# Per-block landing signals for x, and the last gate product taken ahead of the root, in a one-core decoder layer

## The chip, the cores and the metric

The kernel runs on one core of a Trainium2 chip. Its five engines are TensorE (PE, with its weight loads shown apart as PEld), VectorE (DVE), ScalarE (ACT), GpSimd (POOL) and SyncE (SP, which here only issues DMAs). The metric is the device time of one execution in microseconds; lower is better.

## The reference

One decoder layer on 512 tokens (four blocks of 128) of width 1024, in float32:

```
mod = silu(c) @ w_mod + b_mod            # six rows: shift, scale, gate for the mixer and for the FFN
h = rms_norm(x, pre_mix_gain) * (1 + scale_m) + shift_m
y = hybrid_mixer(h, ...)                 # differential attention beside a gated delta rule, one output projection
x = x + gate_m * rms_norm(y, post_mix_gain)
h = rms_norm(x, pre_ffn_gain) * (1 + scale_f) + shift_f
y = peer_ffn(h, ...)                     # 8 heads, product keys, top 16 of 16384 single-neuron experts
x = x + gate_f * rms_norm(y, post_ffn_gain)
```

Two places matter here. The first line with `rms_norm` needs the sum of squares of every row of x. The last line is, for each row, out = x1 + (y * gate) / sqrt(mean(y^2) + eps), where `gate` is gate_f times post_ffn_gain and x1 the x after the mixer.

## The kernel before

All buffers are placed by hand, every engine runs a program written out in order, and engines meet only at semaphores. The matrix products are float32 split in two parts (`hi`, `lo`), so each product is three matmuls.

**The start.** SP issues c (`c_row`), then the four blocks of x into `xn`, three small tables, and then weight tiles of 512 KB each in one stream: modulation tiles 0 to 3, input-projection tiles 0 and 1, modulation tiles 4 to 7, and so on. ACT takes silu(c), loads its table for the root, squares blocks 0 and 1 of x with the row sums kept (`ssq`); DVE squares blocks 2 and 3. All four x DMAs raise one semaphore, `s_x`, and both engines wait for its full count before the first square. ACT then takes the root of the means; DVE multiplies the first modulation tile (`mod_tile(0)`), inverts the roots, scales blocks 2 and 3, while ACT scales blocks 0 and 1. DVE goes on with modulation tiles 1 to 3 and from them makes the columns `acol`, `bcol` (`s_cols`). PE runs ten matmuls of the identity once block 0 is squared (`WARM`, waiting for `s_ssq`), then, when x is scaled, 32 transposes. ACT rounds the first weight tile (`hi(0)`, needs its DMA), copies two transposed column blocks out of PSUM (`x_copied(2)`, `x_copied(3)`) and makes h for the first two (`h_made`: a scale and a bias from `acol`, `bcol`, then a cast). DVE takes the remainders (`low`), and PE starts on the first natural tile of the input projection, 24 matmuls. Its end frees the weight slot for which ACT waits with `hi(2)`.

**The middle** is not touched: attention, delta rule, output projection, x1, retrieval beside the down projection of all 128 expert tiles, up projection of the same tiles for token blocks 0 to 2. Block 3 is done from 128 gathered rows per token on DVE (`ysp`).

**The end.** The blocks are finished in the order `FINISH` = (3, 0, 1, 2); block 3 lies in `ysp`, the other three in two PSUM banks each. PE ends with the last two expert tiles, one bank after the other, and signals each bank with `s_yb`. ACT squares the two halves of a block with row sums (`out_square`) and takes the root when DVE has the mean. DVE does, for each block in `finish(n)`, the following; the two halves are 512 columns each:

```
tt(rstd, ssq2 half 0, ssq2 half 1, add); drain; ts(rstd, 1/D, EPS) -> s_ym     # the mean of squares
wait s_yr; reciprocal(rstd); drain                                             # ACT's root between
for half in range(2):
    stt(yo = y * rstd * gate_f); drain; tt(yo = yo + x1) -> s_yo
```

SP stores blocks 3, 0 and 1 with one DMA of 512 KB each, and block 2 with one of 256 KB for each half.

Of the kernel before, what the change touches and what calls it, by code (L numbers as in the profile page):

```python
# [26 lines left out]
F32 = mybir.dt.float32  # L27
# [4 lines left out]
ALU = mybir.AluOpType  # L32
# [3 lines left out]
P = 128  # L36
D = 1024
SEQ = 512
KD = D // P
NB = SEQ // P  # L40
# [29 lines left out]
NG = NB - 1  # L70
# [24 lines left out]
def build(nc, x, c, mod_tiles, mod_bias_col, gain_cols, in_tiles,  # L95
# [6 lines left out]
    with ExitStack() as ctx:  # L102
        def sem(name):
            return ctx.enter_context(nc.semaphore(name))
# [4 lines left out]
        def at(name, shape, dt, offset=None):  # L109
            size = 2 if dt == BF16 else 4  # L110
            for n in shape[1:]:
                size *= n
            offset = cursor[0] if offset is None else offset
            cursor[0] = offset + (size + 31) // 32 * 32
            assert cursor[0] <= 229344, (name, cursor[0])
            return nc.alloc_sbuf_tensor_at(name, shape, dt, offset=offset)
# [11 lines left out]
        gate_f = at("gate_f", [P, D], F32)  # L128
# [6 lines left out]
        phase = cursor[0]  # L135


        xn = at("xn", [P, NB, D], F32)
# [83 lines left out]
        rstd = small[:, 8:12]  # L222
# [26 lines left out]
        bank = [ctx.enter_context(nc.psum_tensor(f"bank{i}", [P, 512], F32)) for i in range(8)]  # L249
# [43 lines left out]
        asp = at("asp", [P, P], F32)  # L293
        assert cursor[0] <= phase + 32 * 1024
        rows = at("rows", [P, ROWS, D], F32, phase + 32 * 1024)
        x1 = at("x1", [P, NB, D], F32, late)
        yo = at("yo", [P, NB, D], F32)
        ysp = at("ysp", [P, D], F32)
# [5 lines left out]
        s_hi = sem("split_hi_ready")  # L304
        s_lo = sem("split_lo_ready")
        s_used = sem("split_used")
        s_x = sem("x_landed")
        s_crow = sem("c_landed")
        s_c = sem("consts_landed")
        s_hc = sem("head_consts_landed")  # L310
# [120 lines left out]
        s_yq = sem("y_squares")  # L431
        s_yqa = sem("y_first_half_squares")
        s_ym = sem("y_mean_square")
        s_yr = sem("y_root")
        s_yo = [sem(f"out_ready{b}") for b in range(NB)]
        s_out = sem("out_stored")
# [18 lines left out]
        def _(sp):  # L455
            dq = sp.dma_start
            dq(c_row[:], c.partition_broadcast(P)).then_inc(s_crow, 16)
            for b in range(NB):
                dq(xn[:, b, :], x[b]).then_inc(s_x, 16)
            for dst, src in [(gaincol[:], gain_cols), (modbcol[:], mod_bias_col), (baw[:], ba_w)]:  # L460
                dq(dst, src).then_inc(s_c, 16)

# [229 lines left out]
        def _(act):  # L692
# [12 lines left out]
            sc.activation(gate_f[:], c_row[:], ACT.Silu).then_inc(s_cc, 1)  # L705
            act.wait_ge(s_pool, 1)
            sc.activation(rx[:, 0:1], eps_t, ACT.Sqrt)
            act.wait_ge(s_x, 16 * NB)
            for b in range(2):
                sc.activation(qkvT[:, 0:2, :], xn[:, b, :].rearrange("p (a n) -> p a n", a=2),  # L710
                              ACT.Square, accum_out=ssq[:, b:b + 1]).then_inc(s_ssq, 1)
                act.wait_ge(s_ssq, b + 1)
# [347 lines left out]

            def out_square(b, half):
                w = slice(half * 512, (half + 1) * 512)
                return sc.activation(yo[:, b, w], ysp[:, w] if b == NG else bank[2 * b + half][:],
                                     ACT.Square, accum_out=ssq2[:, 2 * b + half:2 * b + half + 1])

            for n, b in enumerate(FINISH):
                for half in range(2):
                    if b < NG:
                        act.wait_ge(s_yb, NB - 1 + 2 * b + half + 1)
                    elif half == 0:  # L1070
                        act.wait_ge(s_axpy, PICKS)
                    last = out_square(b, half)
                last.then_inc(s_yq, 1)
                act.wait_ge(s_ym, NB + n + 1)
                sc.activation(rstd[:, b:b + 1], rstd[:, b:b + 1], ACT.Sqrt).then_inc(s_yr, 1)
# [468 lines left out]
        def _(dve):  # L1544
# [65 lines left out]
                tt(wlo[:, n % SPLIT, :], raw[:, n % RAW, :], whi[:, n % SPLIT, :].bitcast(F32),  # L1610
                   ALU.subtract).then_inc(s_lo, 1)

            dve.wait_ge(s_x, 16 * NB)
            for b in range(2, NB):
                v.tensor_tensor_reduce(out=qkvT[:, 2 * b:2 * b + 2, :].rearrange("p a n -> p (a n)"),
                                       in0=xn[:, b, :], in1=xn[:, b, :], scale=1.0, scalar=0.0, op0=ALU.mult,
                                       op1=ALU.add, accum_out=ssq[:, b:b + 1]).then_inc(s_xsd, 1)
# [540 lines left out]

            def finish(n):
                b = FINISH[n]  # L2160
                dve.wait_ge(s_yq, NB + n + 1)
                tt(rstd[:, b:b + 1], ssq2[:, 2 * b:2 * b + 1], ssq2[:, 2 * b + 1:2 * b + 2], ALU.add)
                v.drain()
                ts(rstd[:, b:b + 1], rstd[:, b:b + 1], 1.0 / D, EPS, ALU.mult, ALU.add).then_inc(s_ym, 1)
                dve.wait_ge(s_yr, NB + n + 1)
                v.reciprocal(rstd[:, b:b + 1], rstd[:, b:b + 1])
                v.drain()
                for half in range(2):
                    w = slice(half * 512, (half + 1) * 512)
                    stt(out=yo[:, b, w], in0=ysp[:, w] if b == NG else bank[2 * b + half][:],  # L2170
                        scalar=rstd[:, b:b + 1], in1=gate_f[:, w], op0=ALU.mult, op1=ALU.mult)
                    v.drain()
                    last = tt(yo[:, b, w], yo[:, b, w], x1[:, b, w], ALU.add)
                    if half == 1 or n == NB - 1:
                        last.then_inc(s_yo[b], 1)

# [64 lines left out]
```

## Time and profile before

| | |
|---|---|
| time, median of 3 runs | 2153.97 us (2153.74 to 2157.31) |
| the profiled execution: own time | 2165.47 us |
| the profiled execution: span from first to last instruction | 2163.4 us |
| busy: PE, PEld, DVE, ACT, POOL | 82%, 66%, 58%, 33%, 40% |
| mean granted TensorE clock | 0.882 of full speed |
| moved by DMA | 376.21 MB, mean 174 GB/s |

The span is 2.1 us shorter than the execution's own time, and that execution was 11.5 us longer than the median. In a row of a timeline the columns are: start and duration in us, engine, line of the kernel, operation, output and inputs with their shapes, how many instructions are merged, and in brackets how long the engine had been idle and what ended that.

### The profile page before, as it was taken

The page shows a single profiled execution, that of the slowest core. Times are in us where ns is not written, and L with a number is a line of the kernel's source. Part 1 is how long each engine was busy: PE and PEld are TensorE (multiplying, and loading weights), DVE is VectorE, ACT ScalarE, POOL GpSimd, SP SyncE. Part 2 cuts the span into 40 slices and gives each one's busy share as a digit, 9 for nine tenths or more (in the row PEclk, how much of TensorE's full clock was granted, in tenths as well). Part 3 has the DMA queues.
Part 4 walks back from the last instruction along what each step waited for, and adds up shares of the span by engine and source line. Part 5 has one row for each costly group of instructions (what it writes and reads, how often), then busy time and mean ns, then how long its engine had stood idle before and what let it go on. Part 6 is the DMA issues. An engine that isn't in the chain of part 4 may idle for free.

```text
span 2163.4 us, 25624 instructions
## 1 busy us (share of the span) xinstructions
PE 1772.3 (82%) x7938; PEld 1419.9 (66%) x7938; DVE 1254.9 (58%) x3054; ACT 704.1 (33%) x1048; POOL 855.5 (40%) x708
## 2 busy tenths in 40 slices
PE   7999899899962279622797227999999999999998
PEld 5776698788841168411585115888888888888886
DVE  7788764316952068610676205722226888888886
ACT  4435654423410034100341002444323333333333
POOL 0332023231077700777007771010005767677750
PEclk9999899999975589755797557999999999999999
DMA  8722913223610034100342003464458999999994
GB/s 344 272 69 95 418 42 108 107 78 127 222 60 15 1 117 146 61 13 15 102 149 69 15 15 102 146 222 142 136 174 286 351 371 360 374 344 372 377 377 160
DMA packets 149363, 376.21 MB, mean 174 GB/s; under 512 B 32048, under 2 KB 64944, under 8 KB 146096
## 3 DMA queue, kind: packets, MB, share of 16 engines
q1 hardware_dynamic: 114480, 308.04, 39.9%
q0 software_dynamic: 34816, 67.41, 8.7%
q8 instruction: 25, 0.41, 0.1%
q14 instruction: 42, 0.34, 0.1%
HBM read 312.25 MB, written 63.11 MB: 174 GB/s over the span
## 4 chain that ended last, share of the span: by engine, by line
PE 76%; issue 17%; DVE 5%; ACT 2%; DMA 1%; DVEq 1%; SPq 0%; ACTq 0%
PE bank L1091 14%; PE bank L1093 14%; PE bank L1092 14%; PE bank L1511 8%; PE bank L1509 8%; PE bank L1513 8%; PE bank L1286 1%; PE bank L1301 1%; DVE modr L1583 1%; PE bank L1469 1%; DVE small L1710 0%; PE bank L1311 0%; DMA xn<-in_x 0%; PE bank L1424 0%; PE bank L1422 0%
## 5 line engine op out<-in xcount | busy, mean ns | idle before, releaser
L1092 PE MATMUL bank<-act_lo,whi 128*128 128x512 f32 x1312 | 530.6, 404 | 115.9 <-issue 115.2
L1093 PE MATMUL bank<-act_hi,wlo 128*128 128x512 f32 x1312 | 529.8, 404 | 115.2 <-issue 114.6
L1091 PE MATMUL bank<-act_hi,whi 128*128 128x512 f32 x1312 | 533.4, 407 | 110.3 <-issue 107.6
L658 POOL DMA_INDIRECT gate_scratch<-merged,idx_cell x384 | 388.3, 1011 | 415.0 <-DVE cand L2039 294.6
L1974 DVE TENSOR_TENSOR wlo<-raw,whi 128x1024 fp32r<-128x1024 f32 x254 | 310.3, 1222 | 411.1 <-ACT whi L1005 365.1
L1093 PEld LDWEIGHTS bank<-act_hi,wlo 128*128 128x128 f32 x1312 | 255.8, 195 | 190.8 <-issue 141.5
L1092 PEld LDWEIGHTS bank<-act_lo,whi 128*128 128x128 f32 x1312 | 256.2, 195 | 185.2 <-issue 137.2
L1091 PEld LDWEIGHTS bank<-act_hi,whi 128*128 128x128 f32 x1312 | 255.8, 195 | 183.6 <-issue 133.6
L1509 PE MATMUL bank<-whi,chi 128*128 128x512 f32 x768 | 298.8, 389 | 0.0
L1511 PE MATMUL bank<-wlo,chi 128*128 128x512 f32 x768 | 298.8, 389 | 0.0
L1513 PE MATMUL bank<-whi,clo 128*128 128x512 f32 x768 | 298.8, 389 | 0.0
L1011 ACT ACTIVATE aout<-bank 128x512 f32<-128x512 f32 x128 | 76.6, 599 | 602.0 <-PE bank L1093 290.9
L667 POOL DMA_INDIRECT asp<-act_scratch,idx_act x128 | 163.1, 1274 | 255.3 <-DMA act_scratch<-aout 216.5
L676 POOL DMA_INDIRECT rows<-in_expert_tiles,idx_row x128 | 176.1, 1376 | 197.8 <-DVE gsp L2017 99.9
L602 POOL TENSOR_TENSOR wlo<-raw,whi 128x1024 fp32r<-128x1024 f32 x38 | 95.8, 2524 | 240.3 <-ACT whi L702 240.3
L1040 ACT CAST chi<-coef 128x384 fp32r<-128x384 f32 x128 | 65.6, 513 | 322.9 <-PE bank L1513 163.2
L2135 DVE SCALAR_TENSOR_TENSOR ysp<-rows,csp,ysp 128x1024 f32<-128x1024 f32 x127 | 163.3, 1286 | 12.1 <-issue 0.4
L1509 PEld LDWEIGHTS bank<-whi,chi 128*128 128x128 f32 x768 | 144.1, 188 | 30.0
L1513 PEld LDWEIGHTS bank<-whi,clo 128*128 128x128 f32 x768 | 144.1, 188 | 29.9
L1511 PEld LDWEIGHTS bank<-wlo,chi 128*128 128x128 f32 x768 | 144.1, 188 | 29.9
L2039 DVE SCALAR_TENSOR_TENSOR cand<-esp,pick 128x128 f32<-128x128 f32 x384 | 113.0, 350 | 79.0 <-issue 77.2
L1005 ACT CAST whi<-raw 128x1024 fp32r<-128x1024 f32 x128 | 133.5, 1043 | 1.0 <-DMA raw<-in_expert_tiles 0.7
(357 smaller groups left out, 1868.9 us busy)
## 6 DMA issues: line engine op xcount, KB each, us to landing
raw<-in_expert_tiles SPq DMA_DIRECT2D x256, 512.0 KB
act_scratch<-aout SPq DMA_DIRECT2D x128, 256.0 KB
gate_scratch<-zeros SPq DMA_DIRECT2D x24, 1024.0 KB, 22.0
a_in<-act_scratch SPq DMA_DIRECT2D x128, 192.0 KB
g_in<-gate_scratch SPq DMA_DIRECT2D x128, 192.0 KB
modr<-in_mod_tiles SPq DMA_DIRECT2D x28, 512.0 KB
raw<-in_in_tiles SPq DMA_DIRECT2D x28, 512.0 KB
raw<-in_query_tiles SPq DMA_DIRECT2D x16, 512.0 KB
```

What stands on the lines that cost most here:

```text
L658: g.indirect_dma_start(out=gate_cells, out_offset=bass.IndirectOffsetOnAxis(ap=idx_cell[:, b, k:k + 1], axis=0), in_=merged[:, b, k:k + 1] ...
L667: g.indirect_dma_start(out=asp[:, k:k + 1], out_offset=None, in_=act_cells, in_offset=bass.IndirectOffsetOnAxis(ap=idx_act[:, k:k + 1], ax ...
L676: g.indirect_dma_start(out=rows[:, k % ROWS, :], out_offset=None, in_=expert_rows, in_offset=bass.IndirectOffsetOnAxis(ap=idx_row[:, k:k + ...
L1005: sc.copy(whi4[:, n % WSLOT, :], raw[:, n % RAW, :]).then_inc(s_hi, 1)
L1091: mm(out_bank[:], whi[:, slot, w], act_hi[:, k, :], start=(k == 0), stop=False)
L1092: mm(out_bank[:], whi[:, slot, w], act_lo[:, k, :], start=False, stop=False)
L1093: last = mm(out_bank[:], wlo[:, slot, w], act_hi[:, k, :], start=False, stop=(k == KD - 1))
L1509: mm(o, chi[:, j % WSLOT, a], whi4[:, j % WSLOT, w], start=start, stop=False, skip_group_check=True)
L1511: mm(o, chi[:, j % WSLOT, a], wlo4[:, j % WSLOT, w], start=False, stop=False, skip_group_check=True)
L1513: return mm(o, clo[:, j % WSLOT, a], whi4[:, j % WSLOT, w], start=False, stop=stop, skip_group_check=True)
L1974: tt(wlo4[:, n % WSLOT, :], raw[:, n % RAW, :], whi4[:, n % WSLOT, :].bitcast(F32), ALU.subtract).then_inc(s_lo, 1)
L2135: stt(out=ysp[:], in0=rows[:, k % ROWS, :], scalar=c, in1=ysp[:], op0=ALU.mult, op1=ALU.add).then_inc(s_axpy, 1)
```

## The change

Two parts. At the start, `s_x` becomes four semaphores, one for each block of x, and each square waits for its own block alone. At the end, DVE first multiplies y by the gate (`by_gate`), the first half as soon as ACT has squared that half (new semaphore `s_ysq`), the second half between handing over the mean and waiting for the root; then one operation for each half multiplies by the inverse root and adds x1. ACT's squares, whose elements nobody reads, go to `ysq`, which lies over the gathered rows, and no longer to `yo`.

```diff
+        ysq = at("ysq", [P, NB, D], F32, phase + 32 * 1024)
...
-                dq(xn[:, b, :], x[b]).then_inc(s_x, 16)
+                dq(xn[:, b, :], x[b]).then_inc(s_x[b], 16)
...
-            act.wait_ge(s_x, 16 * NB)
             for b in range(2):
+                act.wait_ge(s_x[b], 16)
                 sc.activation(qkvT[:, 0:2, :], xn[:, b, :].rearrange("p (a n) -> p a n", a=2),
...
                     last = out_square(b, half)
+                    if half == 0:
+                        last.then_inc(s_ysq, 1)
...
-            dve.wait_ge(s_x, 16 * NB)
             for b in range(2, NB):
+                dve.wait_ge(s_x[b], 16)
                 v.tensor_tensor_reduce(out=qkvT[:, 2 * b:2 * b + 2, :].rearrange("p a n -> p (a n)"),
...
                 b = FINISH[n]
+
+                def by_gate(half):
+                    w = slice(half * 512, (half + 1) * 512)
+                    tt(yo[:, b, w], ysp[:, w] if b == NG else bank[2 * b + half][:], gate_f[:, w], ALU.mult)
+
+                dve.wait_ge(s_ysq, n + 1)
+                by_gate(0)
                 dve.wait_ge(s_yq, NB + n + 1)
                 tt(rstd[:, b:b + 1], ssq2[:, 2 * b:2 * b + 1], ssq2[:, 2 * b + 1:2 * b + 2], ALU.add)
                 v.drain()
                 ts(rstd[:, b:b + 1], rstd[:, b:b + 1], 1.0 / D, EPS, ALU.mult, ALU.add).then_inc(s_ym, 1)
+                by_gate(1)
                 dve.wait_ge(s_yr, NB + n + 1)
                 v.reciprocal(rstd[:, b:b + 1], rstd[:, b:b + 1])
                 v.drain()
                 for half in range(2):
                     w = slice(half * 512, (half + 1) * 512)
-                    stt(out=yo[:, b, w], in0=ysp[:, w] if b == NG else bank[2 * b + half][:],
-                        scalar=rstd[:, b:b + 1], in1=gate_f[:, w], op0=ALU.mult, op1=ALU.mult)
-                    v.drain()
-                    last = tt(yo[:, b, w], yo[:, b, w], x1[:, b, w], ALU.add)
+                    last = stt(out=yo[:, b, w], in0=yo[:, b, w], scalar=rstd[:, b:b + 1], in1=x1[:, b, w],
+                               op0=ALU.mult, op1=ALU.add)
```

DVE's instructions for block 2, the last to be finished, before; `small` holds the sums, means and roots, and what stands in brackets is the semaphore waited for:

```order
L2162 TENSOR_TENSOR small<-small 128x1 [waits y_squares]
L2164 TENSOR_SCALAR small<-small 128x1
L2166 RECIPROCAL small<-small 128x1 [waits y_root]
L2170 SCALAR_TENSOR_TENSOR yo<-bank,small,gate_f 128x512
L2173 TENSOR_TENSOR yo<-yo,x_150 128x512
L2170 SCALAR_TENSOR_TENSOR yo<-bank,small,gate_f 128x512
L2173 TENSOR_TENSOR yo<-yo,x_150 128x512
```

The same place after the change (lines are four to nine further on; a drain is no row):

```order
L2168 TENSOR_TENSOR yo<-bank,gate_f 128x512 [waits y_half_squared]
L2173 TENSOR_TENSOR small<-small 128x1 [waits y_squares]
L2175 TENSOR_SCALAR small<-small 128x1
L2168 TENSOR_TENSOR yo<-bank,gate_f 128x512
L2178 RECIPROCAL small<-small 128x1 [waits y_root]
L2182 SCALAR_TENSOR_TENSOR yo<-yo,small,x_151 128x512 x2
```

There are four wide instructions as before. Two of them now stand ahead of the reciprocal, one ahead of the sum, and the last two follow each other with no drain between.

ACT's first rows after the change, at the start of the program, where only the waits of the two squares (`qkvT,small<-xn`) are new:

```order
L709 ACT_TABLE_LOAD
L709 ACTIVATE small<-small 128x1 [waits pool_consts]
L712 ACTIVATE qkvT,small<-xn 128x1024 [waits x_landed0]
L712 ACTIVATE qkvT,small<-xn 128x1024 [waits x_landed1,sum_of_squares]
L716 ACTIVATE small<-small 128x4 [waits x_squared_then_scaled_by_vector,sum_of_squares]
L719 ACTIVATE xn<-xn,small 128x1024 [waits inverse_root]
```

No instruction moved there; the first square waits for block 0 of x, the second for block 1, where both had waited for all four.

## Rows read from the trace of the kernel before

**Rows 1.** The page's chain of work that ended last, shares of the span.

```profile
PE 76%; issue 17%; DVE 5%; ACT 2%; DMA 1%; DVEq 1%; SPq 0%; ACTq 0%
```

**Rows 2.** That chain in order of time: start us, us, what.

```profile
2.61 7.97 DMA xn<-in_x
...
30.77 0.04 ACT whi L702
```

**Rows 3.** The four DMAs of x (line L459), from issue to landing.

```profile
DMA to landing us min/median/max: 5.3/6.6/8.0
```

**Rows 4.** Timeline, the first 24 us.

```profile
10.60 1.06 ACT L710 ACTIVATE qkvT<-xn 128x1024 f32<-128x1024 f32 x1 [3.02 <-DMA xn<-in_x]
...
11.75 1.22 DVE L1615 CUSTOM_DVE_ANT_0 qkvT<-xn 128x1024 f32<-128x1024 f32 x1
...
11.89 4.59 PE L1113 MATMUL bank<-ident 128*128 128x128 f32 x20 [11.89 <-ACT qkvT L710]
...
12.90 1.22 DVE L1583 CUSTOM_DVE_ANT_0 modr<-modr,gate_f 128x1024 f32<-128x1024 f32 x1
...
16.49 3.48 PEld L1118 LDWEIGHTS bank<-ident,xn 128*128 128x128 f32 x32 [0.29 <-ACT xn L717]
...
17.19 1.05 ACT L702 CAST whi<-raw 128x1024 fp32r<-128x1024 f32 x1 [0.75 <-DMA raw<-in_in_tiles]
...
18.14 1.07 ACT L722 COPY qkvT<-bank 128x512 f32<-128x512 f32 x2
...
19.57 0.16 DVE L1593 SCALAR_TENSOR_TENSOR acol<-acol,gaincol 128x2 f32<-128x2 f32 x1
...
19.90 0.78 ACT L732 ACTIVATE wk<-bank,bcol,acol 128x512 f32<-128x512 f32 x1 [0.69 <-PE bank L1118]
...
23.48 0.76 PE L1104 MATMUL bank<-whi,act_hi 128*128 128x512 f32 x1 [3.27 <-issue]
```

**Rows 5.** Windows: from:to, length, busy us of PE, PEld, DVE, ACT, POOL, clock, DMA share, GB/s.

```profile
20.30:23.40 3.10, 0.00 (x0) 0.00 (x0) 1.97 (x4) 3.04 (x5) 0.00 (x0) 0.96 1.02 408
23.40:27.00 3.60, 3.52 (x9) 2.83 (x10) 3.60 (x6) 2.29 (x6) 0.00 (x0) 0.56 1.03 411
```

**Rows 6.** Timeline of PE behind an idle stretch later on.

```profile
393.12 5.93 PE L1459 MATMUL bank<-ident,xs 128*128 128x128 f32 x28 [6.03 <-DVE xs L1951]
```

**Rows 7.** Timeline of DVE at the end, first of block 0, then of block 2.

```profile
2149.62 0.16 DVE L2162 TENSOR_TENSOR small<-small 128x1 f32<-128x1 f32 x1 [4.16 <-ACT yo L1063]
...
2157.14 0.15 DVE L2162 TENSOR_TENSOR small<-small 128x1 f32<-128x1 f32 x1
...
2157.80 0.16 DVE L2166 RECIPROCAL small<-small 128x1 f32<-128x1 f32 x1 [0.27 <-ACT small L1075]
2158.03 0.75 DVE L2170 SCALAR_TENSOR_TENSOR yo<-bank,small,gate_f 128x512 f32<-128x512 f32 x1
2158.86 0.69 DVE L2173 TENSOR_TENSOR yo<-yo,x 128x512 f32<-128x512 f32 x1
2159.47 0.75 DVE L2170 SCALAR_TENSOR_TENSOR yo<-bank,small,gate_f 128x512 f32<-128x512 f32 x1
2160.29 0.69 DVE L2173 TENSOR_TENSOR yo<-yo,x 128x512 f32<-128x512 f32 x1
```

**Rows 8.** Timeline of ACT at the end, the squares of block 1 and 2, second halves.

```profile
2151.62 0.60 ACT L1063 ACTIVATE yo<-bank 128x512 f32<-128x512 f32 x1 [0.67 <-PE bank L1513]
...
2154.49 0.59 ACT L1063 ACTIVATE yo<-bank 128x512 f32<-128x512 f32 x1
```

**Rows 9.** Timeline of DVE in the mixer's own norm, where x1 is made.

```profile
371.59 0.16 DVE L1912 TENSOR_TENSOR small<-small 128x1 f32<-128x1 f32 x1 [2.02 <-ACT osq L957]
371.83 0.15 DVE L1914 TENSOR_SCALAR small<-small 128x1 f32<-128x1 f32 x1
371.90 0.68 DVE L1924 TENSOR_TENSOR xs<-bank,gate_m 128x512 f32<-128x512 f32 x1
372.49 0.15 DVE L1918 RECIPROCAL small<-small 128x1 f32<-128x1 f32 x1
```

More of the change, by code:

```diff
@@ L306, in build @@
         s_used = sem("split_used")
-        s_x = sem("x_landed")
+        s_x = [sem(f"x_landed{b}") for b in range(NB)]
         s_crow = sem("c_landed")
@@ L433, in build @@
         s_ym = sem("y_mean_square")
+        s_ysq = sem("y_half_squared")
         s_yr = sem("y_root")
@@ L1062, in out_square @@
                 w = slice(half * 512, (half + 1) * 512)
-                return sc.activation(yo[:, b, w], ysp[:, w] if b == NG else bank[2 * b + half][:],
+                return sc.activation(ysq[:, b, w], ysp[:, w] if b == NG else bank[2 * b + half][:],
                                      ACT.Square, accum_out=ssq2[:, 2 * b + half:2 * b + half + 1])
```

## The prediction

> **What bounds the kernel now.** I read the page's chain first. PE carries three quarters of it and DVE a twentieth [rows 1], so for most of the run a faster DVE is worth nothing. The change touches only the first and last dozen microseconds, so those two ends are read on their own.
>
> At the start the chain in order of time begins with the landing of x, from 2.61 to 10.58 us [rows 2]. ACT had been idle for 3.02 us when it began its first square at 10.60 [rows 4]. From there the chain runs through DVE (squares, modulation tiles, columns), ACT's h, DVE's remainder, and PE's first tile of the input projection at 23.48 [rows 4], and it comes back to ACT's rounding of weight tile 2 at 30.77, which waits for the end of that tile [rows 2]. Behind it engines wait for engines, and I found no wait for a stream of tiles that keeps its own time up to the attention stage; a shift of this start should therefore reach the end of the run.
>
> At the end PE is done at about 2154.3, when ACT takes the last square [rows 8], but DVE works on until 2160.98 [rows 7], and the last store can only be issued then. DVE waits 4.16 us for the squares of block 0 and is then busy without a gap but 0.27 us for each root [rows 7]. The end is DVE's.
>
> **The start, part by part.** The four x DMAs take 5.3 to 8.0 us to land [rows 3]; they were issued one after the other, the first at about 1.2 and the last at 2.6. The first thus lands at 6.5 and the last at 10.6, and as they share one stream I put the other two at even steps between, 7.9 and 9.2 (an estimate). Nothing about the DMAs changes. ACT is free at 7.58 (10.60 - 3.02) [rows 4], squares block 0 at 7.6 and block 1 at 8.8. DVE can square block 2 at 9.2 and block 3 from 10.6 to 11.8; before, that second square began at 11.75 [rows 4]. So DVE's chain is 1.15 us earlier: its first modulation tile would start at 11.75 where it was 12.90 [rows 4]. That tile may land a little later than that. Five tiles, the last of them the projection tile for which ACT waits at 17.19 [rows 4], land between 10.6 and 17.1, some 1.3 us each, which puts the first at 11.9. So I take 1.0 us for DVE's lead; bounds 0.5 (a tile that lands late) and 1.15.
>
> Not all of it comes through. The columns are finished at 19.73 (19.57 + 0.16), and ACT begins h at 19.90, after 0.69 us idle [rows 4]. The row puts this down to PE's transposes, but the bank that it needs was done long before; it is the columns. With these at 18.7, ACT is the late one: its rounding at 17.19 waits for its DMA [rows 4], which does not move, and the two copies behind it end at 19.21 [rows 4]. So h starts at 19.2, and the gain is that 0.69 us, with 0.3 us of DVE's lead left over. PE's first tile starts at 22.8. Bounds of this term: 0 (something that I take for hidden is not) and 0.7.
>
> **TensorE's clock at the start.** PE's ten identity matmuls (20 passes) take 4.59 us, 0.23 each, and the 32 transposes behind them 3.48, 0.11 each [rows 4]: PE was at 1.2 GHz, and at 2.4 GHz once the transposes began. Then it was idle 3.27 us [rows 4]; the granted clock reads 0.96 in that stretch and 0.56 in the next [rows 5], which is 1.2 GHz for about 3.3 us. A projection matmul then starts every 0.43 us and later every 0.23; seven or eight of them cost 1.5 us. The change moves the warm-up and not in step with the rest. It waits for block 0's square, now done at 8.7 and not at 11.8, so it runs from 8.8 to 13.4; the transposes, which wait for the scaling, only come 1.0 us earlier, at 15.5. A hole of 2.1 us opens in work that had been without one, and the idle stretch ahead of the first tile grows from 3.27 to about 3.6 us. I take it that neither changes a level: the hole is shorter than the stretch that did, and the first tile runs at 1.2 GHz as before. Term 0; bounds minus 1.5 (a first tile at 2.4 GHz) and plus 3.3 (all its 24 matmuls at 1.2 GHz: 24 x 0.20 = 4.8, less the 1.5 that it loses already).
>
> The Trainium skill, TensorE: Matmul & The Clock Gate, in the part on the HAM clock gate, says that the slow level is the default, that activity releases it and idling brings it back. The granted clock of the idle stretch agrees. By that rule a warm-up that is cut off from its work is partly wasted, and this speaks against the early signal; the second rival below prices it from rows.
>
> **The end, part by part.** Before, a block takes DVE from sum to sum 3.76 us: sum to reciprocal 0.66 with the wait for the root, 0.23 to the first product, 0.83 (drained) to the sum with x1, 0.61 to the second product, 0.82, 0.61 [rows 7]. After, the steps are priced by the mixer's norm, which already has this pattern: sum to mean 0.24, mean to gate product 0.07, product out of PSUM to reciprocal 0.59, with the root already there [rows 9]; reciprocal to the next wide one 0.23 [rows 7]. The two combined operations are not in the trace with a wide one behind them and no drain. They are of the kind of 0.75 us [rows 7], and the undrained one of 0.69 is followed after 0.61 [rows 7], so I take 0.75 - 0.08 = 0.67. With the first gate product at 0.60, a block takes 0.60 + 0.24 + 0.07 + 0.59 + 0.23 + 0.67 + 0.67 = 3.07 us. Is another engine late then? The sum of block 0 waits for ACT's square as before, at 2149.62, and its first gate product fits under ACT's second square. Blocks 0, 1 and 2 end at 2149.62 + 2.47 + 3.07 + 3.07 + 0.08 = 2158.3. ACT's square of block 1's second half ends at 2152.3 and is wanted at 2152.7; that of block 2 ends at about 2155.1 and is wanted at 2155.8 [rows 8]. So DVE stays the bound, 2.7 us earlier than 2160.98. Behind it come the same two stores of 256 KB; they are now issued 0.7 us apart, where it was 1.4, and may queue for 0.1 us. Bounds for the end: 1.9 (the first rival) and 2.8. Block 3 is finished under PE's last matmuls and costs nothing.
>
> **Sum.** 0.7 at the start and 2.7 at the end are 3.4 us: the profiled execution would have a span of 2160.0 and an own time of 2162.1. That execution was 11.5 us over the median, but the two ends are priced by durations that do not hang on it, so I take the 3.4 off the median: 2153.97 - 3.4 = 2150.6 us, or 0.16%. Less than 0.2% (4.3 us) is about what a measurement of this kernel can't tell from no change.
>
> **Rivals.** First, the drain is not what costs. The Trainium skill, VectorE: DVE Perf Modes, Rules for kernel authors, says that an operation waits for the pipe behind the one before it whatever one writes, and that only their number counts; the number of wide ones is unchanged here. The rows speak against it, 0.82 with a drain and 0.61 without [rows 7], though for two kinds of operation. As a mechanism: the combined operations keep 0.82. A block then takes 3.37 us and not 3.07, the end gives 1.9, and the time is 2151.4. Chance 0.08.
>
> Second, the hole costs the clock and gives it back: the transposes run at 1.2 GHz. A transposition pass at that level took 5.93 / 28 = 0.21 us [rows 6]. The four groups that ACT needs then end at 15.5 + 16 x 0.21 = 18.9, the copy behind them at 19.6, and the start gives 0.3. But the transposes end at 21.5 or later, PE is idle under 2 us, and the first tile runs at 2.4 GHz: 1.5 more. Sum 0.3 + 1.5 + 2.7 = 4.5, time 2149.5. Chance 0.25. Close to it, with 0.08: the transposes stay fast and the clock doesn't fall before the first tile, 4.9, 2149.1.
>
> Third, the start gives nothing, since a tile or the ACT queue is later than I read: only the end's 2.7, time 2151.3. Chance 0.12.
>
> Fourth, on the other side: the hole keeps PE at 1.2 GHz through the transposes and the whole first tile. Then the start gives 0.3 and costs 3.3, the end gives 2.7, and the time is 2154.3; if the low level lasts into the second tile, each matmul there adds 0.2, and 20 of them make it slower by over 0.2%. It decides as soon as the low level outlasts the first tile. Against it: 7 us of unbroken transposing raised or held the clock here. Chance 0.05.
>
> **How the numbers follow.** The forecast has 0.42, the rest is above. Faster by over 0.2% needs 4.3 us: most of the second rival and its neighbour, and what a scatter of a microsecond or more (the three runs differ by 3.6) adds to the forecast: 0.32. Slower: half of the fourth rival and a slow draw, 0.05. The rest, 0.63, is within 0.2%. The range takes in 2149.1 and 2154.3, with that scatter on the lower side: 2146.8 to 2154.4.
>
> **What would show it.** Right: ACT's first square at about 7.6 and the PE warm-up at 8.8; h at 19.2 and the first projection matmul at 22.8; at the end, gate products under the squares, no idle time before the reciprocals, 3.1 us from sum to sum, 8.7 us from block 0's sum to the last element where it was 11.36. Wrong: transposes at 0.21 a pass, a first tile at another level than before, a 0.8 step between the combined operations, or a middle between 31 and 2147 us whose length has changed by more than a microsecond: then clock or queues elsewhere, not this change's terms, decide the measured difference.

## The result, and the profile after

| | before | after |
|---|---|---|
| median of 12 runs each | 2154.83 us (2144.95 to 2163.83) | 2151.6 us (2114.15 to 2158.68) |
| the profiled execution: own time | 2165.47 us | 2150.9 us |
| its span | 2163.4 us | 2149.1 us |
| mean granted TensorE clock | 0.882 | 0.887 |

The ratio after to before is 0.9864, with a 95% interval of 0.9824 to 0.9903: faster by 1.0 to 1.8%. The medians of all twelve runs differ by 3.2 us, which is 0.15% and close to the 3.4 us forecast. The ratio and the medians don't agree because the ratio counts only three of the changed kernel's twelve runs (2114.15, 2127.27 and 2135.65), the others lying more than 1.5% above the fastest. The mean of these three lies 27 us below that of the other nine, and the first question is whether that has anything to do with the change.

The start is seen in the timeline of the changed kernel's first 24 us (start, duration, engine, line, operation, idle time before), the counterpart of [rows 4].

```profile
7.76 1.04 ACT L712 ACTIVATE qkvT<-xn 128x1024 f32<-128x1024 f32 x1
...
9.04 4.60 PE L1117 MATMUL bank<-ident 128*128 128x128 f32 x20 [9.04 <-ACT qkvT L712]
...
10.59 1.23 DVE L1619 CUSTOM_DVE_ANT_0 qkvT<-xn 128x1024 f32<-128x1024 f32 x1
...
12.23 1.23 DVE L1587 CUSTOM_DVE_ANT_0 modr<-modr,gate_f 128x1024 f32<-128x1024 f32 x1 [0.41 <-DMA modr<-in_mod_tiles]
...
15.83 3.71 PE L1122 MATMUL bank<-ident,xn 128*128 128x128 f32 x32 [2.19 <-ACT xn L719]
...
18.16 1.06 ACT L724 COPY qkvT<-bank 128x512 f32<-128x512 f32 x2
...
18.90 0.16 DVE L1597 SCALAR_TENSOR_TENSOR acol<-acol,gaincol 128x2 f32<-128x2 f32 x1
...
19.24 0.78 ACT L734 ACTIVATE wk<-bank,bcol,acol 128x512 f32<-128x512 f32 x1
...
22.82 0.47 PE L1108 MATMUL bank<-whi,act_hi 128*128 128x512 f32 x1 [3.28 <-issue]
```

The squares start with their own blocks. The first modulation tile comes 0.67 us earlier than before, not 1.0, for DVE now waits 0.41 us for its DMA. The columns are done at 19.06 and ACT's copies at 19.22, so h starts at 19.24 and the first projection matmul at 22.82, 0.66 us earlier than before. PE has the forecast hole of 2.19 us behind its warm-up. Its transposes take 3.71 us, and took as long before: the 3.48 us of [rows 4] are those of the weight loads (PEld, 3.48 us in both traces), and PE's own row in the kernel before is this one.

```profile
16.50 3.71 PE L1118 MATMUL bank<-ident,xn 128*128 128x128 f32 x32
```

The end is seen in DVE's timeline of the changed kernel, of block 0, the sum of block 1, and block 2, the counterpart of [rows 7].

```profile
2137.99 0.16 DVE L2173 TENSOR_TENSOR small<-small 128x1 f32<-128x1 f32 x1 [0.67 <-ACT ysq L1065]
2138.23 0.15 DVE L2175 TENSOR_SCALAR small<-small 128x1 f32<-128x1 f32 x1
2138.30 0.68 DVE L2168 TENSOR_TENSOR yo<-bank,gate_f 128x512 f32<-128x512 f32 x1
2138.90 0.15 DVE L2178 RECIPROCAL small<-small 128x1 f32<-128x1 f32 x1
2139.13 1.42 DVE L2182 SCALAR_TENSOR_TENSOR yo<-yo,small,x 128x512 f32<-128x512 f32 x2
...
2141.06 0.15 DVE L2173 TENSOR_TENSOR small<-small 128x1 f32<-128x1 f32 x1
...
2144.12 0.15 DVE L2173 TENSOR_TENSOR small<-small 128x1 f32<-128x1 f32 x1
...
2145.02 0.15 DVE L2178 RECIPROCAL small<-small 128x1 f32<-128x1 f32 x1
2145.25 1.41 DVE L2182 SCALAR_TENSOR_TENSOR yo<-yo,small,x 128x512 f32<-128x512 f32 x2
```

From sum to sum it is 3.07 and 3.06 us, no reciprocal waits for its root, and from block 0's sum to the last element it is 8.67 us (2145.25 + 1.41 - 2137.99) where it was 11.36. This is the forecast to a hundredth or two.

The middle did not repeat. I cut each trace at PE's matmuls number 3000 (about 604 us in), 4400 and the last, by their starts in the timeline:

| us | start to 3000 | 3000 to 4400 | 4400 to the last | last to the end |
|---|---|---|---|---|
| before | 606.2 | 747.8 | 799.9 | 9.5 |
| after | 603.7 | 738.6 | 799.9 | 6.8 |

The end part is 2.7 us shorter. The part up to matmul 3000 is 2.5 us shorter, of which the first projection matmul accounts for 0.66. But 9.2 of the 14.3 us between the two spans lie between matmuls 3000 and 4400, where both programs are the same. What goes on there is seen in windows of the changed kernel (from:to, length, busy us of PE, PEld, DVE, ACT and POOL, granted clock, DMA share, GB/s).

```profile
590.00:610.00 20.00, 20.00 (x90) 16.58 (x89) 19.46 (x118) 5.39 (x6) 15.73 (x15) 1.00 0.35 114
610.00:640.00 30.00, 17.00 (x37) 9.22 (x36) 12.79 (x65) 4.46 (x5) 23.00 (x24) 0.58 0.18 53
640.00:770.00 130.00, 28.92 (x50) 14.34 (x50) 18.93 (x82) 4.34 (x5) 88.53 (x91) 0.50 0.05 13
770.00:790.00 20.00, 20.00 (x79) 16.26 (x79) 16.66 (x77) 8.82 (x10) 0.00 (x0) 0.87 0.48 156
```

GpSimd scatters the gates of a token block here, one indirect DMA per pick, 128 for each of three blocks. For 25 us (90 matmuls in 20 us) PE doesn't feel it. Then every engine but POOL nearly stops: 50 matmuls in 130 us, with the clock at 1.2 GHz, until shortly after the block's last scatter. The timeline of all engines in that stretch has about one matmul and one weight load on PE every 2.8 us, and one instruction on DVE every 1.4 (POOL's rows, a scatter every 1.27 us, are left out).

```profile
664.73 0.29 DVE L1987 MAX8 top<-S 128x8 f32<-128x128 f32 x1 [1.10 <-issue]
664.76 0.59 PE L1097 MATMUL bank<-act_hi,wlo 128*128 128x512 f32 x1 [1.53 <-issue]
...
666.13 0.29 DVE L1987 MAX8 top<-S 128x8 f32<-128x128 f32 x1 [1.10 <-issue]
666.15 0.29 PEld L1095 LDWEIGHTS bank<-act_hi,whi 128*128 128x128 f32 x1 [1.81 <-issue]
...
667.53 0.29 DVE L1987 MAX8 top<-S 128x8 f32<-128x128 f32 x1 [1.11 <-issue]
667.55 0.59 PE L1095 MATMUL bank<-act_hi,whi 128*128 128x512 f32 x1 [2.20 <-issue]
```

"Issue" is all that the trace says on the wait. It isn't a wait for full DMA engines, whose share is 0.05 in that window. The same stall comes with each of the three blocks. My prediction did not look there.

### The profile page after: what moved, and what is told of

It is laid out like the page before. It is cut to its first block, busy times and chain, and to the rows that moved or that the text cites. A ratio compares the mean times of both kernels' runs of the same rounds, so it can differ in the third digit from the quotient of the medians.

```text
span 2149.1 us, 25617 instructions
## 1 busy us (share of the span) xinstructions
PE 1764.1 (82%) x7938; PEld 1417.5 (66%) x7938; DVE 1249.9 (58%) x3054; ACT 703.9 (33%) x1048; POOL 852.1 (40%) x708
## 4 chain that ended last, share of the span: by engine, by line
PE 76%; issue 17%; DVE 5%; ACT 2%; DMA 1%; DVEq 1%; SPq 0%; ACTq 0%
PE bank L1095 14%; PE bank L1097 14%; PE bank L1096 14%; PE bank L1513 8%; PE bank L1517 8%; PE bank L1515 8%; PE bank L1290 1%; PE bank L1305 1%; DVE modr L1587 1%; PE bank L1473 1%; DVE small L1714 0%; PE bank L1315 0%; PE bank L1428 0%; PE bank L1426 0%; PE bank L1427 0%
```

## Experiments

The theory was that the change is worth its two ends, some 3.4 to 4.5 us, and that the short runs are an accident of the three scatter stretches. Its rival (theory B in the expectations) was that the change itself makes the short runs.

**The parts, and both kernels again.** On one chip, beside 35 runs of the kernel before (median 2152.71, 2125.11 to 2162.5), 12 runs of each. The first is the changed kernel itself, the last the kernel before against itself.

> The changed kernel once more, unaltered. Theory A (the two ends give 0.7 and 2.7 us, and whatever makes single executions 20 to 40 us shorter lies in the middle and is not the change's): most executions 3.4 us below the kernel before, 2149 to 2153, and short ones (under 2140) at most as often as chance has it, in both kernels. Theory B (the change itself makes the short executions): again about a quarter of the executions under 2140, and none of before.

Measured: 2147.58 us (2131.62 to 2155.34); ratio 1.0016 [0.9975, 1.0057].

The start alone keeps the four signals and takes the end of before:

```diff
-                    last = stt(out=yo[:, b, w], in0=yo[:, b, w], scalar=rstd[:, b:b + 1], in1=x1[:, b, w],
-                               op0=ALU.mult, op1=ALU.add)
+                    stt(out=yo[:, b, w], in0=ysp[:, w] if b == NG else bank[2 * b + half][:],
+                        scalar=rstd[:, b:b + 1], in1=gate_f[:, w], op0=ALU.mult, op1=ALU.mult)
+                    v.drain()
+                    last = tt(yo[:, b, w], yo[:, b, w], x1[:, b, w], ALU.add)
```

> Only the per-block signals of x; the end as before. Theory A: 0.7 us below before in the span of undisturbed parts (first projection matmul at 22.8 and not 23.5), median 2153 to 2154, not to be told from before. Theory B, if the start is what makes the short executions (it shifts everything behind it against the clock's steps): short ones here and none in the end's part.

Measured: 2147.67 us (2120.91 to 2155.02); ratio 0.9981 [0.9932, 1.003].

The end alone puts the one semaphore for x back:

```diff
-                act.wait_ge(s_x[b], 16)
+            act.wait_ge(s_x, 16 * NB)
...
-                dve.wait_ge(s_x[b], 16)
+            dve.wait_ge(s_x, 16 * NB)
```

> Only the gate product ahead of the root; the start as before. Theory A: from block 0's sum to the last element 8.7 us and not 11.4; median 2.7 us below before, 2151 to 2152. Theory B, if the end is what makes the short executions (it cannot act before 2140 us, but it moves buffers): short ones here.

Measured: 2137.04 us (2108.92 to 2154.94); ratio 0.9894 [0.9836, 0.9952]. This is 14 us below what theory A said, and 7 of its 12 runs are under 2140 us.

> The kernel before against itself. Both theories: ratio 1.000. Theory A: with enough executions one or more short ones under 2140 us appear here too, since they have nothing to do with the change. Theory B: none. The spread tells how wide a median of so many executions is.

Measured: 2142.03 us (2121.59 to 2155.82); ratio 0.9952 [0.9906, 0.9998].

The kernel before is "faster than itself" by an interval that leaves out 1, and the changed kernel, 1.4% faster in the first comparison, is not faster here by the same kind of ratio. So such intervals are too narrow for this kernel. Under 2140 us are 3 of 12 runs of e1, 3 of e2, 5 of e4 (the kernel before) and 8 of the 35 beside them, so theory B, which wanted none of the kernel before, falls. The 7 of 12 of e3 were not repeated; e1 has the same end and only 3. Repeated on two more chips later:

> The kernel before, whole, on another chip or the same. The last call timed the whole kernel before at 1732.7 us where the first chips gave 2152. Theory D (the three scatter stretches stall the other engines on some chips only): the time is either about 1733 with executions within 5 us, and then the profile shows PE at its pace of 0.23 us a matmul while GpSimd scatters, or about 2150 with a spread of 40, and then matmuls 2.8 us apart in the three stretches. Rival: something between, which would speak for a gradual cause.

> The changed kernel, whole, in the same call. Theory A: on a chip of about 1733 us, 3.4 to 4.5 us below the kernel before, as with the scatters left out (4.2 there), a ratio of about 0.9977. On a chip of 2150 us the same difference, hidden in the spread.

> The changed kernel, whole and unaltered. If the kernel before reads 1733 us in this call: 1729 to 1730, a ratio of 0.9975 to 0.998, that is 3.4 to 4.3 us (theory A). If it reads 2153: a spread of 40 us again and a median 0 to 5 us lower, which says nothing more.

Measured: the kernel before 2153.35 us (2126.4 to 2158.97), ratio 0.9984 [0.9934, 1.0033]; the changed one 2153.07 (2110.12 to 2157.3) and 2149.11 (2126.65 to 2158.71), the latter 1.0022 [0.9968, 1.0076]. All such runs, the result's and e1's, e4's, e9's, e10's and e17's with those of the kernel before beside them, taken together: before, 103 runs, median 2152.7, standard deviation 10.8; after, 42 runs, median 2150.6, deviation 11.9. The medians differ by 2.1 us (95%: 6.0 faster to 0.6 slower). Under 2140 us are 20 of the 103 and 10 of the 42. With such a scatter, 3 us can't be resolved in the whole kernel, and a small effect of the change on the stall can't be excluded either.

The traces locate the scatter (us, cut as above):

| | start to 3000 | 3000 to 4400 | 4400 to the last | last to the end |
|---|---|---|---|---|
| changed kernel: e1, e10, e17 | 604.0, 603.1, 603.3 | 719.1, 737.5, 746.9 | 799.9 each | 6.8 each |
| e2, start only | 603.5 | 730.1 | 799.9 | 9.5 |
| e3, end only | 603.6 | 716.8 | 799.9 | 6.8 |
| kernel before: e4, e9 | 604.5, 604.0 | 725.2, 733.7 | 799.9 each | 9.5 each |

Every trace with the new end has 6.8 and every one with the old end has 9.5. The part from 3000 to 4400 spreads over 23 us for the kernel before (with the first trace) and 28 for the changed one. It depends on how long the scatters run before the stall sets in: in e1's windows it has only begun at 640 us, where in the trace above PE was already nearly stopped.

```profile
640.00:660.00 20.00, 14.37 (x55) 9.71 (x53) 11.07 (x59) 4.71 (x6) 15.43 (x16) 1.00 0.25 73
660.00:700.00 40.00, 9.69 (x17) 4.96 (x18) 6.33 (x26) 1.03 (x2) 30.55 (x32) 0.54 0.08 20
```

**The change without the scatters.** These four issue one scatter in eight; the gates of the other picks of token blocks 0 to 2 are left out, so that part of the FFN isn't computed.

```diff
+                    if k % SKIP:          # SKIP = 8
+                        continue
                     g.indirect_dma_start(
                         out=gate_cells,
```

> The kernel before with one scatter in eight of the gates (48 of 384, the other gates of token blocks 0 to 2 are left out of the result). Theory A (the spread of 20 to 50 us lies in the three stretches in which GpSimd scatters): the three stretches shrink from about 160 us to about 20 each, the time falls by several hundred us at most and by over 150 at least, and the executions agree within 2 us. Rival C (the spread comes from elsewhere, PE's clock or the weight stream): the executions still differ by 20 us or more.

> The changed kernel with the same scatters left out. Theory A: 3.4 us below the kernel before in the same form (0.7 at the start, 2.7 at the end), with a spread small enough to see it; 2.4 to 4.4 with the clock's steps at the start. Theory B (the change does more than its two ends, by 20 us): 10 us or more below.

> Only the per-block signals, same scatters left out. Theory A: 0.7 us below the kernel before in the same form, with up to 1.5 either way from the clock in the first projection tile. Theory B: 10 us or more.

> Only the end's part, same scatters left out. Theory A: 2.7 us below the kernel before in the same form. The rival that a drain costs nothing: 1.9. Theory B: 10 us or more.

Measured, ten runs each, beside 31 runs of the whole kernel before:

| | median us | range | ratio |
|---|---|---|---|
| whole kernel before | 1732.74 | 1730.59 to 1735.1 | |
| e5, before | 1733.31 | 1732.42 to 1734.44 | 1.0004 [0.9995, 1.0014] |
| e6, both parts | 1728.56 | 1727.71 to 1730.29 | 0.9978 [0.9968, 0.9987] |
| e7, start only | 1732.04 | 1730.39 to 1733.07 | 0.9996 [0.9986, 1.0006] |
| e8, end only | 1729.56 | 1727.89 to 1731.54 | 0.9985 [0.9975, 0.9994] |

Two results. The surprise stands in the first line: on this chip the whole kernel before, with all its scatters, takes 1732.7 us and not 2153, so here leaving scatters out saved nothing. And where nothing stalls, a kernel's runs lie within 2 to 5 us (rival C falls: all four traces have 317.3 us between matmuls 3000 and 4400), and the change shows: by the means, both parts together are 3.8 us below the whole kernel and 4.5 [3.6, 5.3] below e5, the end alone 2.9 and 3.6, the start alone 0.9 and 1.6. Only the start alone is not clear of no change against the whole kernel (its ratio takes in 1). The parts add up (1.6 + 3.6 = 5.2 against 4.5, within the intervals).

**Is the hole worth filling? Is the drain the price?** Both without seven scatters of eight (the same gates left out), on a chip where the kernel before has a median of 2156.51. The first fills PE's idle time behind the transposes with ten more identity matmuls, the second puts a drain behind each combined operation.

```diff
+            pe.wait_ge(s_xcp, 1)
+            for _ in range(KEEP):         # KEEP = 10
+                mm(bank[2][:, 0:P], ident[:], ident[:], start=True, stop=True)
```

> The changed kernel with seven of eight scatters left out and ten more identity matmuls on PE behind the transposes, which fill most of the 3.3 us ahead of the first projection tile. If TensorE's clock at the start is priced right (1.5 us for a first tile at 1.2 GHz), the first tile always runs at 2.4 GHz and the executions gather at the fast end, 1728 or up to 1.5 below the same kernel without them (median 1728.6); if the transposes at 1.2 GHz are what costs, or what is added delays the first tile, 1729 to 1731.

```diff
                     last = stt(out=yo[:, b, w], in0=yo[:, b, w], scalar=rstd[:, b:b + 1], in1=x1[:, b, w],
                                op0=ALU.mult, op1=ALU.add)
+                    v.drain()
```

> The changed kernel, the same scatters left out, with a drain behind each combined operation of the end. Theory A (a drained wide operation is followed after 0.82 us, an undrained one after 0.67): both steps between the combined operations go from 0.66 to about 0.82, 0.8 us more over the last three blocks. The rival (a drain costs nothing): no step changes.

Measured: 1727.99 us (1727.58 to 1729.13) and 1730.01 us (1728.84 to 1740.25; one of its five runs is 8 us long from 1220 us on, away from the edit). Both are some 427 us below the whole kernel on the same chip: seven eighths of the scatters are what the stall hangs on. The fill gives 0.6 us at most against e6, across two chips; that isn't shown, and at the start it changed nothing: the first projection matmul is at 23.46 us and the 25th at 29.00, in e6 at 23.47 and 29.03. The drain is in DVE's timeline of e12, first of block 0:

```profile
1726.17 0.16 DVE L2176 TENSOR_TENSOR small<-small 128x1 f32<-128x1 f32 x1 [0.67 <-ACT ysq L1068]
...
1727.31 1.58 DVE L2185 SCALAR_TENSOR_TENSOR yo<-yo,small,x 128x512 f32<-128x512 f32 x2
...
1729.59 0.15 DVE L2176 TENSOR_TENSOR small<-small 128x1 f32<-128x1 f32 x1
...
1732.99 0.15 DVE L2176 TENSOR_TENSOR small<-small 128x1 f32<-128x1 f32 x1
```

and without it in e6:

```profile
1717.23 0.16 DVE L2176 TENSOR_TENSOR small<-small 128x1 f32<-128x1 f32 x1 [0.67 <-ACT ysq L1068]
...
1718.36 1.41 DVE L2185 SCALAR_TENSOR_TENSOR yo<-yo,small,x 128x512 f32<-128x512 f32 x2
...
1720.29 0.15 DVE L2176 TENSOR_TENSOR small<-small 128x1 f32<-128x1 f32 x1
```

A block takes 3.42 and 3.40 us with two drains and 3.06 without: 0.17 us for each drain, and the pair 1.58 for 1.41. From the last matmul to the end it is 7.7 us where e6 has 6.8.

**Fewer scatters under way.** Nothing is left out here. The kernel lets up to 16 scatters be under way (two groups of SGROUP = 8); these allow 2 or 4.

```diff
-SGROUP = 8
+SGROUP = 1        # e13, e14 (the kernel before), e16 (with the ten matmuls of e11)
+SGROUP = 2        # e15, e18
```

> The changed kernel, nothing left out, but a scatter waits until the last but one has landed (at most 2 under way, 16 before). Theory E (many scatters under way at once make the stall of all engines, and its irregular beginning makes the spread): no stall, about 1730 us and a spread of a few us, if the 384 scatters, now some 1.4 to 1.9 us each and so 540 to 730 in all, are still done before the up projection asks for the gates. Rival F (the sheer number of scatters makes it): still above 2100.

> The kernel before with the same limit. Theory A: 3.4 to 4.5 us above e13, as with the scatters left out, with nothing left out here. Theory B (the change does more): 10 us or more.

> The changed kernel with at most 4 scatters under way. Theory E with a threshold above 4: like e13, about 1730. With a threshold between 2 and 4, or rival F: above 2000.

> e13 with ten more identity matmuls behind the transposes, to keep TensorE's clock up ahead of the first projection tile. From the run with scatters left out (1728.0 against 1728.6): 0 to 1 us below e13, the fastest version.

Measured, on a chip where the kernel before takes 1733.02 us (1732.28 to 1734.85, 12 runs): e13 1824.93 (ratio 1.053), e14 1832.26, e15 1729.31 (1728.07 to 1730.6; 0.9976 [0.9966, 0.9986]), e16 1827.36. With two under way the scatters are spun out until 1269 us and the up projection waits for their gates: in e13's window PE is busy 17.84 of 110 us.

```profile
1190.00:1300.00 110.00, 17.84 (x66) 14.18 (x65) 8.88 (x13) 6.77 (x11) 70.58 (x73) 0.57 0.26 90
```

So e13's forecast of 1730 failed for want of time for the scatters, e13 and e14 carry another bound, and their difference of 7.3 us, which theory A had put at 3.4 to 4.5, isn't the change's price: of the 8.7 us between their traces, 4.2 lie between matmul 4400 and the last, where the gates are waited for. e16 has no gain over e13. e15 is the nearest to the change in the whole kernel on a chip that repeats: 3.7 us below before. It differs from it by two edits, the change and the limit of 4; the limit shows no cost of its own, for its trace has the parts of the traces without the scatters (317.3 and 799.9 us). The change unaltered was run on no such chip. Its windows, beside those of the changed kernel above, have no stall:

```profile
610.00:640.00 30.00, 30.00 (x134) 24.88 (x133) 29.65 (x168) 13.64 (x16) 23.63 (x21) 1.00 0.41 141
640.00:770.00 130.00, 130.00 (x576) 107.75 (x575) 121.32 (x541) 53.98 (x63) 99.17 (x89) 1.00 0.45 146
```

GpSimd does the same here as there (89 and 91 scatters in 130 us, most of them 1.27 us apart), but PE has 576 matmuls where it had 50. Is that the limit of 4 (theory E), or the chip (rival F)? The same kernel on a chip where the kernel before has a median of 2152.09:

> The changed kernel with at most 4 scatters under way. On a chip where the kernel before takes 2153 us, theory E: 1730 here. Rival F (the chip, whatever the number under way): 2100 or more here too. On a chip of 1733 us: 1729 again.

Measured: 2139.27 us (2096.21 to 2145.97). The stall is back, seen in e18's windows:

```profile
610.00:640.00 30.00, 22.77 (x66) 13.49 (x65) 20.15 (x102) 6.29 (x7) 22.27 (x21) 0.77 0.26 79
640.00:770.00 130.00, 40.78 (x82) 20.43 (x81) 17.22 (x92) 6.08 (x8) 91.53 (x92) 0.54 0.07 19
```

Theory E falls for a limit of 4: what decided was the chip, or something else that held for all runs made on it together, as each chip was measured on one occasion only. The medians of the kernel before are 1733 us on two of the five chips and 2152 to 2157 on three, with nothing between, as theory D had it. Two under way wasn't tried on a chip that stalls.

## Where the prediction failed, and what of it was right

**The step that failed.** The forecast was a gain of 0.16%, too small to tell from no change, and the comparison measured 1.0 to 1.8%. What failed is the step that turns the sum into a result, in "How the numbers follow": the scatter of single executions is put at "a microsecond or more" and the middle at nothing. The runs showed a standard deviation of 11 us, and a middle (matmuls 3000 to 4400) of 717 to 748 us for the same instructions; three executions of 2114 to 2136 us make the measured ratio. A second step, the level of TensorE's clock at the start, failed too and didn't decide the result. The terms of the end were right.

**The end was right, term and mechanism.** 2.7 us forecast, 9.5 to 6.8 in every pair of traces, 2.9 to 3.6 in the times of e8. The first rival is refuted: a block took 3.07 us and not 3.37, and e12 measures 0.17 us for each explicit drain put back. The rule named with it, the Trainium skill, VectorE: DVE Perf Modes, Rules for kernel authors (the wait for the pipe comes whatever one writes), does not speak of an explicit drain instruction, and here that instruction has a price of its own.

**The start, near 0.7 by luck.** In the result's trace h and the first matmul were where I put them, and rival 4 did not occur in any trace. The step that failed is "I take it that neither changes a level", the term of 0. The warm-up cut off from its work did cost the clock; the profiled execution of the result happened to be the one exception. In e1's timeline of PE and ACT:

```profile
8.89 4.61 PE L1117 MATMUL bank<-ident 128*128 128x128 f32 x20 [8.89 <-ACT qkvT L712]
...
15.79 6.31 PE L1122 MATMUL bank<-ident,xn 128*128 128x128 f32 x32 [2.29 <-ACT xn L719]
...
18.65 0.59 ACT L724 COPY qkvT<-bank 128x512 f32<-128x512 f32 x1 [0.43 <-PE bank L1122]
...
19.50 0.59 ACT L724 COPY qkvT<-bank 128x512 f32<-128x512 f32 x1 [0.27 <-PE bank L1122]
...
19.98 0.78 ACT L734 ACTIVATE wk<-bank,bcol,acol 128x512 f32<-128x512 f32 x1
...
23.57 0.47 PE L1108 MATMUL bank<-whi,act_hi 128*128 128x512 f32 x1 [1.47 <-issue]
```

and in e3's of PE, where the warm-up is late and runs on into the transposes:

```profile
11.82 4.60 PE L1117 MATMUL bank<-ident 128*128 128x128 f32 x20 [11.82 <-ACT qkvT L712]
16.42 4.12 PE L1122 MATMUL bank<-ident,xn 128*128 128x128 f32 x32
23.41 0.47 PE L1108 MATMUL bank<-whi,act_hi 128*128 128x512 f32 x1 [2.87 <-issue]
```

In 10 of the 11 traces with the early signal (the two with the fill are not counted) the transposes take 5.38 to 6.67 us, up to 0.21 a pass, and in all ten the first tile then runs at 2.4 GHz. In six of them (e1, e6, e7, e12, e13, e15) this delays ACT's copies, as above, so that h starts at 19.9 to 20.2 us and the first projection matmul at 23.5 to 23.8, no earlier than with the late signal (23.4 to 23.7); in the other five of the eleven it is at 22.7 to 22.8. So the 0.66 us of the first matmul came in five of eleven, and in the rest rival 3's "the start gives nothing" held for it. With the late signal the transposes take 3.71 to 4.19 us, and six of seven traces have 1.2 GHz in part of the first tile. The 25th projection matmul starts at a median of 29.1 us with the early signal and 30.6 with the late one. That is rival 2, to which I gave 0.25, though it had put the copies' end at 19.6 where six traces have 20.0 to 20.3. The rule named there, the Trainium skill, TensorE: Matmul & The Clock Gate, HAM clock gate (the slow level is the default, and idling brings it back), was the better guide: these traces agree in kind, with the pace of 0.21 us behind a hole of 2.3. Its 1.5 us more didn't stay: nine of the eleven have a stretch at 1.2 GHz near 211 us (0.79 mean clock in e1's window from 209 to 217 us, 1.00 in e3's), which only two of the seven have. At matmul 3000 the means are 603.8 and 604.5 us; single traces spread over 2.6 us on each side, so these 0.7 us aren't shown by them. The times of e7 say 0.9 and 1.6, by its two references. That the start is worth what I forecast is luck: a loss and a gain of the clock that I had both left out. The stretch near 211 us goes with a first tile at 2.4 GHz (10 of 11 traces, with either signal; 1 of the 7 others); why is open.

**DVE's lead** was 0.67 us, not 1.0: modulation tile 0 landed near 12.2 us, not at the 11.9 worked out from even steps. h didn't lose by it, as the copies set its start.

**The sum** of 3.4 us measured 3.7 (e15), 3.8 and 4.5 (e6, by its two references) where runs repeat: from the forecast to rival 2. The 3.2 of the first medians lies so near by luck, with 12 runs on each side and a deviation of 11.

**The scatter was the error that decided.** I took it for "a microsecond or more", since the three runs before lay within 3.6 us. The profiled execution's 11.5 us over the median, which I noted and set aside, was the sign. The standard deviation is 11 us. The range held the median, but the chance of 0.63 for "within 0.2%" was worked out as if the comparison could tell it: by the ratio, the result is faster by 1.4%, and with both kernels run again it is nothing. The last point of "what would show it" did name this case, a middle whose length changes by more than a microsecond, and that is what decides the measured ratio.

**What stays open:** why every engine's issue nearly stops under the scatters on three chips (and in the result's runs) and not on two others, though e15 and e18 are one and the same program, and whether it is the chip or the occasion. It takes a flow of scatters (with one in eight it is gone) and allowing 4 under way in place of 16 doesn't cure it; whether it matters where the scattered cells lie, or whether instructions reach the engines late, wasn't tried.

No version run beats the changed kernel clearly. Its two nearest forms (e6 and e15) are 0.22 and 0.24% faster than the kernel before where that takes 1733 us. Where the scatters stall, the same microseconds would be 0.17%, an estimate that no comparison there resolves.

## What to carry to other kernels

Put the product that doesn't need a statistic ahead of the root, and join what is left into one operation: 0.7 us for each of the first two blocks and 1.3 for the last, as the durations of single instructions had said. A warm-up that is cut off from its work can leave that work at the low level (6.3 us of transposes in e1 where 4.1 in e3) and still leave the next piece at the high one; when a signal is moved, look at what the engine's idle time does to both neighbours, in more than one trace. Before forecasting a few microseconds of two thousand, look for stretches where all engines are slow at once and compare the profiled execution with the median: if these differ by more than the change is worth, it takes a kernel without that stretch, or a chip on which it doesn't occur, to measure it.

## What the runs showed of the hardware

- A stream of indirect scatters of single floats from GpSimd, one per 1.27 us, nearly stopped the other engines on three chips (in the result's trace a matmul every 2.8 us on PE and an instruction every 1.4 on DVE). It cost 420 of 2153 us over three stretches (matmuls 3000 to 4400 took 717 to 748 us, and 317.3 in e15 and in e5 to e8). On two chips it did nothing, with the same instruction stream. From 640 to 770 us the DMA engines were 5% busy in the result's trace, with the stall, and 45% in e15's, without it.
- The onset of that stall varies from one execution to the next: the stalled part of the trace spreads over 31 us and a kernel's time over some 50 us (2110 to 2164), while in the whole kernels' traces the part before it repeats to 4 us and the parts behind it to 0.1.
- A drain behind a 128x512 float32 vector operation cost 0.17 us (e12 against e6).
- A pass of the transposes took 0.11 us at 2.4 GHz and up to 0.21 at 1.2 GHz. The granted clock read 1.00 over e1's slow transposes (window 15.6 to 22.4 us), though 25 of the 31 steps between them are of 0.21 us or more, the pace of the lower level: the column seems to hold only from the record's first change of level on, so early in a program the pace is the better witness.
